# Differential attention on one Trainium2 core: the two short context units of a chunk stand fourth and eighth instead of last

## The reference, cut to what matters

```python
def diff_attention(q1, q2, k1, k2, v, lam):
    s1 = jnp.einsum('bqhd,bkhd->bhqk', q1, k1).astype(jnp.float32) * ATTN_SCALE
    s2 = jnp.einsum('bqhd,bkhd->bhqk', q2, k2).astype(jnp.float32) * ATTN_SCALE
    w = jax.nn.softmax(s1, axis=-1) - lam * jax.nn.softmax(s2, axis=-1)
    return jnp.einsum('bhqk,bkhe->bqhe', w, v.astype(jnp.float32))
...
    ob_x = blocked_diff_attention(q1x, q2x, [k1x, k1c], [k2x, k2c], [vb_x, vb_c], lam)
    ob_c = diff_attention(q1c, q2c, k1c, k2c, vb_c, lam)
```

## Time and profile before

| | |
|---|---|
| median of three runs | 3389.41 us (3389.07 to 3390.85) |
| the profiled execution's own time | 3399.27 us |
| its span | 3397.5 us |
| PE busy, share of the span | 2881.9 us, 85% |
| DVE busy | 1676.6 us, 49% |
| ACT busy | 1235.1 us, 36% |
| the stage in question | from about 752 us to about 1070 us of the span |

### The profile page before, as it was taken

The page is one execution under the profiler, slowest core; times in us unless marked ns, Lnnn a source line. Parts: engine busy times, 40 slices in busy tenths (PEclk is TensorE's granted clock), DMA queues, the critical chain, the costliest instruction groups (busy, mean ns, idle before and its releaser), DMA issues. The chain is left out here.

```text
span 3397.5 us, 36082 instructions
## 1 busy us (share of the span) xinstructions
PE 2881.9 (85%) x13812; PEld 2250.5 (66%) x13812; DVE 1676.6 (49%) x2712; ACT 1235.1 (36%) x1984; POOL 168.9 (5%) x253
## 2 busy tenths in 40 slices
PE   5999997967776999996986999999899588678883
PEld 1767885636665878883654799977666466457772
DVE  3566445637776340105653356432144353567885
ACT  3545212434554231113432231112234311257776
POOL 0000000100000000000000000000000010011112
PEclk9999998978998989995887999999999779879997
DMA  5233433245203032221114123332242441379996
GB/s 216 92 124 131 162 128 94 73 133 137 70 16 109 19 112 103 84 75 70 66 55 168 45 76 110 106 99 87 88 111 71 122 124 56 121 264 366 380 371 246
DMA packets 145791, 431.58 MB, mean 127 GB/s; under 512 B 20002, under 2 KB 46370, under 8 KB 144340
## 3 DMA queue, kind: packets, MB, share of 16 engines
q1 hardware_dynamic: 101636, 265.08, 23.5%
q0 software_dynamic: 26704, 93.80, 8.2%
q10 hardware_dynamic: 17280, 70.39, 5.7%
HBM read 322.74 MB, written 106.47 MB: 126 GB/s over the span
## 5 line engine op out<-in xcount | busy, mean ns | idle before, releaser
L1055 PE MATMUL acc<-act_hi,w_hi 128*128 128x512 f32 (+3 forms) x2512 | 738.7, 383 | 120.4 <-DVE act_lo L834 64.5
L1055 PE MATMUL acc<-act_lo,w_hi 128*128 128x512 f32 (+3 forms) x2512 | 712.7, 373 | 0.0
L1055 PE MATMUL acc<-act_hi,w_lo 128*128 128x512 f32 (+3 forms) x2512 | 709.9, 372 | 0.0
L1055 PEld LDWEIGHTS acc<-act_hi,w_hi 128*128 128x128 f32 x2512 | 456.0, 192 | 234.3 <-issue 77.9
L739 DVE TENSOR_TENSOR w_lo<-w_stage,w_hi 128x1024 fp32r<-128x1024 f32 x126 | 154.3, 1225 | 796.6 <-ACT w_hi L570 796.5
L1055 PEld LDWEIGHTS acc<-act_lo,w_hi 128*128 128x128 f32 x2512 | 454.7, 193 | 79.0
L1055 PEld LDWEIGHTS acc<-act_hi,w_lo 128*128 128x128 f32 x2512 | 452.6, 192 | 80.1
L570 ACT ACTIVATE w_hi<-w_stage 128x1024 fp32r<-128x1024 f32 x126 | 133.3, 1058 | 961.7 <-PE acc L1055 920.0
L2668 DVE TENSOR_TENSOR expert_lo<-expert_stage,expert_hi 128x1024 fp32r<-128x1024 f32 x186 | 225.8, 1223 | 78.7 <-ACT expert_hi L2605 76.4
L2605 ACT ACTIVATE expert_hi<-expert_stage 128x1024 fp32r<-128x1024 f32 x186 | 195.8, 1057 | 93.2 <-DMA expert_stage<-in_exp_w 46.4
L1831 DVE TENSOR_REDUCE max<-scores 128x1 f32<-128x256 f32 (+6 forms) x256 | 117.3, 484 | 149.6 <-PE scores L1955 148.7
(11 more groups left out here) (395 smaller groups left out, 4121.5 us busy)
## 6 DMA issues: line engine op xcount, KB each, us to landing
expert_stage<-in_exp_w SPq DMA_DIRECT2D x186, 512.0 KB, 6.6
w_stage<-in_w_in SPq DMA_DIRECT2D x43, 512.0 KB, 4.3
rope<-out_stage ACTq DMA_DIRECT2D x26, 640.0 KB, 3.6
proj<-out_stage ACTq DMA_DIRECT2D x26, 640.0 KB, 5.3
slots_out<-residual POOLq DMA_DIRECT2D x31, 512.0 KB, 6.7
w_stage<-in_ab_w_in SPq DMA_DIRECT2D x26, 512.0 KB, 4.8
w_stage<-in_gla_w_in SPq DMA_DIRECT2D x25, 512.0 KB, 4.9
residual<-in_adaln_w POOLq DMA_DIRECT2D x24, 512.0 KB, 3.8
```

The costliest lines, as they stand in the source:

```text
L1055: mmi = eng.matmul(a[:, t, 0:n], lhs[:, j.w % 2, kb:kb + P], rhs[:, c0 + k, off:off + n], start=first, stop=last)
```

## The change

The list of a chunk's units is written in another order. The context units 8 and 9 stood at places 8 and 9 (counted from 0); they now stand at places 3 and 7.

```diff
-                        P1[18 + c], P1[22 + c], O1[4 + c], [Unit(0, P * i, *qblocks(i, False)) for i in range(10)])
+                        P1[18 + c], P1[22 + c], O1[4 + c], [Unit(0, P * i, *qblocks(i, False)) for i in (0, 1, 2, 8, 3, 4, 5, 9, 6, 7)])
```

## The result

The changed kernel took 3398.66 us, the median of seven runs (3395.88 to 3406.7), beside 3389.41 for the kernel before (3381.28 to 3391.14): a ratio of 1.0038 with a 95% interval of 1.0025 to 1.0051. Two further sets of twelve runs each gave 1.0019 (1.0005 to 1.0033) and 1.0021 (1.0009 to 1.0034). The kernel is slower, by less than half a per cent. Single runs of one and the same kernel scatter by about 5 us (standard deviation), so I also took means over all sets: 3397.2 for 31 runs of the changed kernel, 3389.8 for 88 runs of the one before, 7.4 us more, give or take 2. The forecast was 3391.8 with a range of 3382 to 3399.5 and a chance of 0.67 for no measurable change.

The account below looks back on a forecast made before the run. All-long steps were taken as bound by VectorE plus the head of TensorE's step. Chunks +1.1 - 2.2 - 1.0 + 3.8 = +1.7, plus 0.7 for a chance fall: +2.4 on 3389.41, 3391.8 us, range 3382 to 3399.5.

Parts of the forecast that it names:

- LSL step: Step with a long unit's transposes and products, a short unit's difference and long scores; forecast 6.55 us.
- SLL step: Step with a short unit's two transposes at its head, then long difference and long scores; forecast 7.38 us without values.
- LLL behind an SLL step: All-long step after the short unit's pause, during which the clock comes back; forecast 8.8 us instead of 7.61.
- LLS behind that: Step with short scores following that all-long step, bound by TensorE with ScalarE's copies; forecast 5.64 us.
- LLL with four value blocks at half clock: All-long step at place 8 with four value blocks ahead of its transposes; 8.8 + 1.96 = 10.76 us.
- drain: End of the last chunk, now two long units instead of two short; 13.3 us full clock, 16.3 half, 14.5 taken.
- clock falls behind SLL steps: TensorE's clock falls in every SLL step, two per chunk: eight falls where there were three.
- chance fall: Fall in the second chunk's old LLS step with no long wait ahead, 1.6 us; 0.7 us allowed for recurrence.
- Rival 1: Clock holds in the SLL steps: 9.7 us less, 3382.1 us; chance 0.12.
- Rival 2: Half clock outlasts the LLL step into the LLS step at place 5: 6.4 us more, 3398.2 us; chance 0.12.
- Rival 3: LSL step no shorter than LLL, as TensorE starts late behind LLS: 8.5 us more, 3400.3 us; chance 0.07.
- Rival 4: Recurring short pauses in LLL steps make the clock fall; ten falls fewer, 16 us, giving 3376; chance 0.02.

Follow-up runs that it names:

- fill_tail: Against the kernel before: new order in three chunks, old in the fourth, 24 useless matmuls in each pause behind a short unit; ratio 0.9972, stage 306.15 us.
- before_again: The kernel before, run again without an edit as a single traced execution; its gated products stage took 116.1 us.

## Why the prediction was wrong

The kinds of steps and the falls came as the prediction put them, and the steps at full clock nearly to the last digit. The numbers from the trace after:

| term | forecast, us | measured, us |
|---|---|---|
| LSL step | 6.55 | 6.52 to 6.56 |
| SLL step | 7.38 | 7.39, 7.39, 7.40, 7.40, 7.39 |
| SLL with four value blocks | 9.22 | 9.23 |
| LLL with two value blocks | 8.95 | 8.94, 8.95 |
| LLL behind an SLL step | 8.80 | 9.04, 9.12, 9.34, 8.94 |
| LLS behind that | 5.64 | 5.80, 6.00, 6.00, 5.64 |
| LLL with four value blocks at half clock | 10.76 | 11.17, 11.00, 11.00 |
| drain | 14.5 | 15.0 |
| clock falls behind SLL steps | 8 | 8 |

What failed is the price of the half clock. The mechanism stood: eight falls, one behind each SLL step, and a longer drain. But four terms were too small, all on one side: the LLL step behind a pause (1.2 us too little in all), the LLS step behind that one (0.9), the LLL step with values (0.9) and the drain (0.5). Together that is 3.5 us over the +1.7 of the sum, which gives the 5.2 between the two first traces (323.2 less 318.0). Against the average stage of before it is the +5.5 measured, where I had said +2.4 with 0.7 for a chance fall that this trace does not have. With the kernel's mean loss of 7.4 us that carries it past the 6.8 us that I had called the edge of what can be told, and the median of the first set, 3398.66, lies near the top of the range, on the side for which I had given 0.19. Of the 9 us by which the first medians differ, the stage explains 5.5.

The LLL step behind a pause was read from the wrong rows. I took 8.8 from two steps of before that began with transposes of 0.63 and 0.95 us, so with some of their head still at full clock. Behind the longer pause the clock was down before the step began: the four transposes take 1.08 or 1.09 us. (In the later traces the fall did not always come so early, and such steps took from 8.13 to 9.35 us.) The third boundary of before, which I did not read, had that already: its step began at 926.01 with transposes of 1.08 and took 9.04 us. One step of each kind in the windows view, of before and of after; the PEclk is 0.81 and 0.68:

```profile
1004.11:1013.01 8.90, 7.74 (x43) 6.79 (x44) 6.31 (x14) 4.63 (x10) 0.00 (x0) 0.81 0.00 0
```

```profile
954.27:963.61 9.34, 8.77 (x43) 7.80 (x44) 6.29 (x13) 4.21 (x9) 0.00 (x0) 0.68 0.00 0
```

In the four such steps of after the granted clock is 0.73, 0.70, 0.68 and 0.84. The LLL step with values was built on the same 8.8 and is short for the same reason. In the drain it is the first step: 7.07 us, where I had put 5.1 at full clock and 6.6 at half.

The LLS step behind that one is a term that I had read from the wrong neighbour. I took 5.64 from steps that began with a wait. Behind an LLL step at half clock TensorE does not wait: it begins the moment its own work is done, when ScalarE still has the long second exponential ahead of the copy of the first group. In the trace after, ScalarE beside the step that begins at 885.37:

```profile
885.38 1.31 ACT L1330 ACTIVATE probs<-scores,stats 128x1280 f32<-128x1280 f32 x1
...
886.59 0.19 ACT L1330 ACTIVATION_READ_ACCUMULATOR probs<-scores,stats 128x1 f32 x1
886.68 0.58 ACT L1319 ACTIVATE probs_t<-transposed 128x512 f32<-128x512 f32 x1
```

The copy begins 1.31 us into the step, and the second group of transposes waits for it; in the LLS step of before that starts at 973.16 it begins 0.95 in. That is the 0.36 us. It comes in the second and third chunk. In the first the copy begins 1.11 us into the step, which makes 0.16, and in the fourth the clock came back earlier and TensorE waited again (8.94, then 5.64).

Rival 1, that the clock would hold, did not come true once in eight pauses. Rival 2, that the half clock would last into the LLS step, did not come true: the granted clock of these steps is 1.00. What it stood for, that the LLS step feels the fall, came by another way and at under a quarter of the price, handed on through ScalarE. Rival 3 did not show. Rival 4, that the recurring short pauses make the clock fall, did not show in this trace. But the sum called the fall in the LLS step of the second chunk a chance that comes once, and it is in all three traces of before. It is also why the second chunk alone came out shorter, by 1.3 us: without it that chunk would have lost 0.3.

The count of falls in the prediction, eight where there were three, makes the old order look better than it is. At each boundary of before the clock was low in the SLL step (granted 0.66 to 0.67) and again in the LLL step behind it (0.80 to 0.82). The sum is not touched, since the chunks of before were taken as measured.

The first judgement that I would change is the one on scatter. The three runs shown beforehand lay within 1.8 us, and I took the profiled execution, 10 us off, as an oddity. The kernel before ranges from 3377 to 3401 us over all its runs, and the gated products alone, over all traces, from 113 to 120 us with the clock. A change of 5 us in one stage can be read from traces of that stage, from single runs of the kernel it can't.

## What to carry to other kernels

When short work is spread among long work to balance one engine, ask what the others do meanwhile: here each spread short unit left TensorE without work for 4 us, and its clock was then at 1.2 GHz for a good part of the next long step. Look at keeping short units at the end of a pipeline: here they shortened the drain. Price a step by the neighbours it will have, since a step that begins after a wait and one that begins without differ, and one that begins with the clock already down costs more than one in which it falls. If a pause can't be avoided, useless matmuls in it can pay for themselves: with them both orders came out faster in the stage than they were, the old one by 7.7 us and the new one by 11.4.

## What the runs showed of the hardware that I had not expected

Twenty-four matmuls of 128x256 in bf16 that nobody reads, 2.8 us of TensorE's time, kept the clock up at no cost in time: SLL steps of 7.40 with them and of 7.39 without. The filled pause left 1.33 us of standing still and no fall; behind the unfilled ones of before, 3.03 to 3.21 us, the clock fell in all of the first trace's three.

Long waits are not the only thing that brings the clock down. In fill_tail it fell within the step that starts at 984.53, behind waits of 0.90 and 0.92 us (the granted clock of that step is 0.83); in the LLS step of before that starts at 893.48 (0.76) it fell behind waits of 1.08 and 0.72 us. In other traces the same places had no fall. What decides it these runs do not show.

The clock of a stage with many small waits, the gated products, is granted differently from one execution to the next: 0.80 and 0.85 in two traces of the same kernel, before and before_again, with 120.1 and 116.1 us.
